# First layer: where the scale and shift rows lie, and when two experts' down weights are loaded

## The reference, cut to what matters

```python
hx = hx + g1x * merge_branches(..., w_out[l])          # output projection, gated residual
u  = rmsnorm(hx, norm2_g[l]) * (1 + sc2x) + sh2x       # scale and shift rows
hb = silu(xb @ w_gate[e]) * (xb @ w_up[e])             # xb: the rows of u given to expert e
y  = (hb @ w_down[e]) * weight
hx = hx + g2x * y
```

## Time and profile before

| what | value |
|---|---|
| median of the runs | 2652.45 us (2652.15 to 2654.38, 3 runs) |
| the profiled execution's own time | 2659.47 us |
| its span (first to last instruction) | 2657.7 us |
| TensorE busy / VectorE busy | 2424.9 us (91%) / 1075.4 us (40%) |
| bytes moved by DMA | 588.27 MB |
| mean granted TensorE clock | 0.979 |

### The profile page before, as it was taken

The page is one execution under the profiler, slowest core; times in us unless marked ns, Lnnn a source line. Parts: engine busy times, 40 slices in busy tenths (PEclk is TensorE's granted clock), DMA queues, the critical chain, the costliest instruction groups (busy, mean ns, idle before and its releaser), DMA issues. The chain is left out here.

```text
span 2657.7 us, 35289 instructions
## 1 busy us (share of the span) xinstructions
PE 2424.9 (91%) x12944; PEld 1516.8 (57%) x12944; DVE 1075.4 (40%) x2132; ACT 622.3 (23%) x1369; POOL 691.2 (26%) x644
## 2 busy tenths in 40 slices
PE   7989988999999999988887899989999999988887
PEld 2445665455555566555554568645787555555553
DVE  5764477444221573111111165854432732322222
ACT  3441222343111232221111142334211311111111
POOL 0003222465231002222222223246531022222221
PEclk8999999999999999999999999999999999999999
DMA  9873030020222529999999913112135689999996
GB/s 365 343 316 137 1 121 19 13 55 1 67 53 87 228 112 361 392 400 401 402 394 385 357 68 113 40 32 55 37 83 178 257 333 393 391 408 407 401 403 246
DMA packets 190670, 588.27 MB, mean 221 GB/s; under 512 B 47376, under 2 KB 109115, under 8 KB 134108
## 3 DMA queue, kind: packets, MB, share of 16 engines
q1 hardware_dynamic: 166053, 551.86, 54.9%
q0 software_dynamic: 22400, 29.42, 3.4%
q10 hardware_dynamic: 2103, 5.51, 0.5%
HBM read 581.31 MB, written 51.51 MB: 238 GB/s over the span
## 5 line engine op out<-in xcount | busy, mean ns | idle before, releaser
L2624 PE MATMUL ps<-w,moe_xt 128*64 128x256 f32 x2816 | 338.3, 394 | 64.4 <-DMA w<-in_w_up_e 61.9
L2764 POOL DMA_INDIRECT rows_out<-moe_rows_out,table x128 | 118.0, 922 | 740.2 <-DVE moe_rows_out L2829 373.9
L2624 PEld LDWEIGHTS ps<-w,moe_xt 128*64 128x64 f32 x2816 | 218.8, 141 | 153.2 <-issue 70.6
L2879 DVE TENSOR_TENSOR moe_gated<-ps,moe_gated 64x256 f32<-64x256 f32 x128 | 54.5, 426 | 504.2 <-ACT moe_gated L2848 504.1
L2848 ACT ACTIVATE moe_gated<-ps 64x256 f32<-64x256 f32 x128 | 48.2, 376 | 668.7 <-PE ps L2624 668.7
L2624 PE MATMUL ps<-early_w,moe_xt 128*64 128x256 f32 x1280 | 151.4, 390 | 31.9 <-DMA early_w<-in_w_up_e 31.8
L1673 POOL TENSOR_SCALAR attn_p<-attn_p,attn_rs 128x768 f32<-128x768 f32 (+1 forms) x80 | 155.4, 1950 | 81.4 <-DVE attn_rs L1847 80.9
L2632 PE MATMUL ps<-w,moe_ht 128*64 128x512 f32 x704 | 170.4, 604 | 2.3 <-issue 2.3
L2145 PE MATMUL ps<-w_out,mix 128*128 128x512 f32 x320 | 144.6, 602 | 7.0 <-PEq L150 7.0
L2865 DVE TENSOR_TENSOR moe_rows_out<-ps,moe_row_gate 64x512 f32<-64x512 f32 x128 | 88.1, 688 | 138.0 <-PE ps L2632 136.0
L2624 PEld LDWEIGHTS ps<-early_w,moe_xt 128*64 128x64 f32 x1280 | 101.3, 140 | 68.3 <-issue 36.6
(11 more groups left out here) (429 smaller groups left out, 4260.5 us busy)
## 6 DMA issues: line engine op xcount, KB each, us to landing
w<-in_w_gate_e SPq DMA_DIRECT2D x88, 1024.0 KB, 25.5
w<-in_w_up_e SPq DMA_DIRECT2D x88, 1024.0 KB, 29.5
w<-in_w_down_e SPq DMA_DIRECT2D x88, 1024.0 KB, 29.3
prep_w<-in_w_ada SPq DMA_DIRECT2D x24, 2048.0 KB, 14.3
early_w<-in_w_gate_e SPq DMA_DIRECT2D x40, 1024.0 KB, 25.5
early_w<-in_w_up_e SPq DMA_DIRECT2D x40, 1024.0 KB, 29.6
early_w<-in_w_down_e SPq DMA_DIRECT2D x40, 1024.0 KB, 29.8
w_merge<-in_w_in SPq DMA_DIRECT2D x32, 512.0 KB, 5.4
```

Source lines behind the costliest of these rows:

```text
L2624: last = nc.tensor.matmul(ps[k * SLOTS:(k + 1) * SLOTS, 0:DE], xt[:, c], wgu[:, k, c], start=c == 0, stop=c == KC - 1)
L2764: nc.gpsimd.indirect_dma_start(out=dram["y"], out_offset=bass.IndirectOffsetOnAxis(ap=m.table[0:SLOTS, j:j + 1], axis=0), in_=y[:, j % 2], ...
L2879: nc.vector.tensor_tensor(h[:, b % 2], m.ps[SLOTS:2 * SLOTS, b % 2, 0:DE], sg[SLOTS:2 * SLOTS, b % 2], ALU.mult).then_inc(s["h_done"], 1)
```

## The change

The out stage's tile `g` is split: the gate row stays in a small tile `gate`, and the scale and shift rows move into a tile `rows` that lies at the top of memory, over the fourth slot. In the first layer that slot now is an early one: its down weights are loaded once the last product by `w_out` is done, its gate and up weights once VectorE has used the rows for the last time (`utok_done`). The down weights of slots 4 and 5, which the out stage loaded after `u_out`, are issued at the start of the moe stage in both layers, and SP's wait for `g1` is gone. TensorE gets 26 instead of 16 `keep_warm` calls at the end of the out stage, and in the moe stage 6 ahead of the first transposes and 4 behind them instead of 4 ahead.

```diff
@@ out_stage, SP
-                    sp.dma_start(s["g"][:, t, k], of(t)).then_inc(s["rows_in" if k else "gates_in"], 16)
+                    sp.dma_start(rows[:, t, k - 1] if k else s["gate"][:, t], of(t)).then_inc(s["rows_in" if k else "gates_in"], 16)
...
             sp.wait_ge(s["mm_done"], 2 * NT)
             freed(sp, 0)
-            sp.wait_ge(s["u_out"], 16 * NT)
+            sp.wait_ge(s["utok_done"], NT)
             freed(sp, 1)
@@ out_stage, TensorE, its end
             lists(NT - 1)
-            keep_warm(nc, m, 0, 16)
+            keep_warm(nc, m, 0, 26)
@@ out_stage, VectorE (gate, gained, rows)
-    ... s["g"][:, t, 0, cols(half)] ... s["g"][:, t, 1, cols(half)] ... s["g"][:, work[j][0], 2]
+    ... s["gate"][:, t, cols(half)] ... rows[:, t, 0, cols(half)] ... rows[:, work[j][0], 1]
@@ moe_stage, SP
-            sp.wait_ge(s["g1"], 16)
             first_loads(sp)
             next_gate_up(RU, 0)
@@ moe_stage, TensorE
+            keep_warm(nc, m, 7, 6)
+            x_transposes(0, 0, 0)
             keep_warm(nc, m, 7, 4)
-            x_transposes(0, 0, 0)
             rounds(pe, body, late_lists)
@@ experts
             def freed_loads(sp, k):
                 if k == 0:
+                    for b in range(early, FREED_EXPERTS):
+                        load_down(sp, a, l, b, slots[b], down_in[b])
                     load_gate_up(sp, a, l, FREED_EXPERTS, slots[FREED_EXPERTS], gu_in[FREED_EXPERTS])
                 else:
-                    for b in (FREED_EXPERTS, RU - 1):
-                        load_down(sp, a, l, b, slots[b], down_in[b])
+                    for b in range(early, FREED_EXPERTS):
+                        load_gate_up(sp, a, l, b, slots[b], gu_in[b])
+
+            def last_downs(sp):
+                for b in (FREED_EXPERTS, RU - 1):
+                    load_down(sp, a, l, b, slots[b], down_in[b])
...
+                rows = until_rows.enter_context(nc.sbuf_tensor(f"out_rows{l}", [P, len(streams), 2, D], F32, side="right"))
...
-        moe_stage(..., lambda sp: first_round(sp, range(early, FREED_EXPERTS)), (xg_at, xg, gathered), out)
+        moe_stage(..., last_downs, (xg_at, xg, gathered), out)
```

More of the change, by code:

```diff
@@ L2093, in out_loads, with out_stage @@
         eng.dma_start(w[:, g], w_out[l].rearrange("(c p) n -> p c n", p=P)[:, :, g * 4 * P:(g + 1) * 4 * P]).then_inc(loaded[g], 16)
-def out_stage(nc, m, l, dram, streams, early, picks, first_rows, gathered, router_loads, then, freed_tiles, freed):
+def out_stage(nc, m, l, dram, streams, early, picks, first_rows, gathered, rows, router_loads, then, freed_tiles, freed):
     work = [(t, at // P + j) for t, at, n in streams for j in range(n // P)]
@@ L2308, in gate @@
                     dve.wait_ge(s["added"], done)
-                nc.vector.tensor_tensor(s["t"][:], m.ps[:, 2 * (j % 2) + half], s["g"][:, t, 0, cols(half)], ALU.mult).then_inc(s["prod_done"], 1)
+                nc.vector.tensor_tensor(s["t"][:], m.ps[:, 2 * (j % 2) + half], s["gate"][:, t, cols(half)], ALU.mult).then_inc(s["prod_done"], 1)
                 dve.wait_ge(s["prod_done"], done + 1)
@@ L2328, in gained, with finished_rows @@
                 dve.wait_ge(s["added"], 2 * j + half + 1)
-                nc.vector.tensor_tensor(s["utok"][:, cols(half)], m.resid[:, tile, cols(half)], s["g"][:, t, 1, cols(half)], ALU.mult).then_inc(s["gained"], 1)
-            def rows(j):
+                nc.vector.tensor_tensor(s["utok"][:, cols(half)], m.resid[:, tile, cols(half)], rows[:, t, 0, cols(half)], ALU.mult).then_inc(s["gained"], 1)
+            def finished_rows(j):
                 dve.wait_ge(s["gained"], 2 * j + 2)
-                nc.vector.scalar_tensor_tensor(s["utok"][:], s["utok"][:], s["r"][:, j:j + 1], s["g"][:, work[j][0], 2], ALU.mult, ALU.add).then_inc(s["utok_done"], 1)
+                nc.vector.scalar_tensor_tensor(s["utok"][:], s["utok"][:], s["r"][:, j:j + 1], rows[:, work[j][0], 1], ALU.mult, ALU.add).then_inc(s["utok_done"], 1)
             def constants():
@@ L2437, in _ @@
                 root(j)
-                rows(j)
+                finished_rows(j)
             selection(NT - 1)
@@ L3115, in experts @@
                 picks[name] = until_moe.enter_context(nc.sbuf_tensor(f"pick_{name}{l}", shape, F32))
-            for b in range(FREED_EXPERTS, RU):
+            for b in range(early, RU):
                 slot_at[b] = top - (RU - b) * SLOT * 4
@@ L3132, in experts @@
             gathered = nc.alloc_semaphore(f"first_rows_in{l}")
-            out_stage(nc, m, l, dram, streams, out_early, picks, xg, gathered, lambda sp: router_loads(sp, l, a, consts, picks),
-                      lambda sp: first_round(sp, range(early)), freed_tiles, freed_loads)
+            with ExitStack() as until_rows:
+                rows = until_rows.enter_context(nc.sbuf_tensor(f"out_rows{l}", [P, len(streams), 2, D], F32, side="right"))
+                assert early == FREED_EXPERTS or nc.sbuf_top == slot_at[early]
+                out_stage(nc, m, l, dram, streams, out_early, picks, xg, gathered, rows, lambda sp: router_loads(sp, l, a, consts, picks),
+                          lambda sp: first_round(sp, range(early)), freed_tiles, freed_loads)
             late.close()
@@ L3141, in experts @@
         homes = blend_homes(nc, l, slot_at, base, top, out is not None)
-        moe_stage(nc, m, l, a, dram, (slots, gu_in, down_in), homes, streams, picks, lambda sp: first_round(sp, range(early, FREED_EXPERTS)), (xg_at, xg, gathered), out)
+        moe_stage(nc, m, l, a, dram, (slots, gu_in, down_in), homes, streams, picks, last_downs, (xg_at, xg, gathered), out)
     return None if out is not None else {"at": (base, top), **{name: homes[name] for name in ("u", "w_hy", "w_hy_in")}}
```

2 lines of the change are left out of this document (1 added, 1 removed).

## The result

The changed kernel's median is 2658.61 us over 12 runs (2652.46 to 2664.73), beside 2653.03 us for the kernel before over 12 runs (2650.16 to 2658.46). The ratio is 1.0019, with a 95% interval of 1.001 to 1.0028: 5.0 us slower, between 2.7 and 7.4. The forecast was 2649.2, 3.25 us faster, in a range up to 2654.5. In a second timing the changed kernel gave 1.0014 (0.9999 to 1.0028).

What follows compares the result with a forecast made beforehand. Each moe stage was taken to end with its stream of loads. First layer 2.2 - 0.2 = 2.0, second 2.6 - 1.35 = 1.25, total 3.25 us gained: 2652.45 becomes 2649.2, range 2645.0 to 2654.5.

Steps and rivals of the forecast that it cites:

- the price of the moved down loads: Moe stage's start: expert 1's gather lands behind the down loads, stalling TensorE 0.2 us in the first layer, 1.35 in the second.
- the gather of 2121.44: Kernel before, second layer: expert 0's gather, landing 7.45 us behind the down loads' issue; the row used to price expert 1's gather.
- the holes behind the stream's start: First layer: the load queue runs dry by about 0.2 and 0.5 us behind expert 6's gate, 0.7 in the sum.
- 7.85 us of bytes: First layer: expert 3's three loads, 3.146 MB, leave the moe stage's stream, worth 7.85 us at 401 GB/s.
- The first layer's boundary: Out stage to moe stage: ten more warm-up calls, 2.4 us, move it from 996.07 to 998.5, TensorE arriving last.
- The first load of the stream: First layer's moe stage: expert 6's gate is issued at 1005.85 instead of 1000.87, 4.98 us later.
- The second layer's boundary: Out stage to moe stage: without the down loads, expert 0's gather lands sooner; boundary at 2126.1 instead of 2126.92.
- rival C: Gather for expert 1 costs its upper bound, stalls of 2.6 and 2.8 us; 0.6 us lost, 2653.0; chance 0.15.
- B's first half: Gather for expert 1 is never late; no stall adds 1.55 us to the gain, 2647.6; whole rival's chance 0.25.
- B's second half: TensorE's clock doesn't fall in the first layer's warm-up calls, adding 1.6 us, 2647.6; whole rival's chance 0.25.
- D: First layer's last store and expert 0's gather stick in 5.24 MB; boundary 7.5 us later, 2656.7; with E, chance 0.10.
- E: Stream isn't the bound; removed bytes give nothing, TensorE's later start costs 3.1 us in the first layer; with D, chance 0.10.

Runs made afterwards that it cites:

- slot-only kernel: Changed kernel with the down loads of slots 4 and 5 back in the out stage in both layers and the previous kernel's warm-up calls; ratio 1.0018.
- warm-up as before: Changed kernel with the warm-up calls of the kernel before (16 at the out stage's end, 4 ahead of the first transposes, none behind); ratio 1.0003.
- the kernel with the wait put back: Changed kernel with SP again waiting for the gather for expert 1 before it issues the two down loads; ratio 0.9999.
- warm-up-only kernel: Kernel before with only the warm-up calls of the changed kernel; ratio 1.0014.
- the down loads alone: Kernel before with only the two down loads moved to the moe stage's start and SP's wait for the gather removed; ratio 1.002.

## Why the prediction was wrong

**The step that failed** is the price of the moved down loads: "I take the 0.2 and 1.35, since here the loads ahead are two and not a full queue." The stalls were 2.1 to 2.5 us in the first layer and 2.6 to 3.1 in the second, over four profiles. That is about the upper bounds of that part, 2.6 and 2.8. I had the right mechanism and put it behind the wrong row: the gather of 2121.44 is alone in its queue, while behind the boundary three gathers are issued within 4 us. All three were held up and went together, so the first of them landed 9.6 us behind the boundary and not 7.45, and in the second layer 9.95 and not 8.6.

The traces have the lone case four times, a gather for expert 0 issued 2.1 to 2.4 us behind the two down loads, and it took 5.1 to 5.7 us. The first of three gathers, issued 2.2 us behind them, took 7.0 to 7.6. That the two others delay the first one's landing is argued from this and from the packet counts and was not tried by itself. Another cause is possible in the second layer, where expert 6's loads are issued at 2131.01, ahead of the landing at about 2133.6; in the first layer SP's queue had a share of only 10% from 1003 to 1004.

The stall works through a second term of the sum, the holes behind the stream's start, which I had put at 0.7 us. In the first profile the hole from 1010 on alone is 2.3 us (3 us at a share of 0.24). In the second, where the clock also fell, it is 4.8:

```profile
1012.00:1018.00 6.00, 6.00 (x38) 3.48 (x34) 5.26 (x7) 0.97 (x2) 0.00 (x0) 0.79 0.20 59
```

So of the 7.85 us of bytes 4.64 went to the later start, and the holes took most of the rest.

**A term was missing.** Behind a stall of 2 us and more TensorE's clock fell, and then expert 1's products took 1.3 to 2.4 us longer: in seven of the eight stretches. The rows of the kernel before had shown this after another wait (5.35 us), and I used that row only for what it gives back. Stall and fall together delay expert 7's loads. In the second layer they are issued at 102.4 on average before (101.9 to 103.3) and at 104.5 after (103.6 to 105.5), 2.1 us later, although the stage begins earlier; the stretch grew by 3.0.

**What was right.** The first layer's boundary: 2.4 us later was forecast, and it was 2.1 (127.03 against 124.93 behind the stage's start). The first load of the stream: 4.98 us later was forecast; counted from the stage's start it was 134.37 against 129.73, 4.64 (3.8 between the means of all profiles). The second layer's boundary is freed by the missing down loads, and GpSimd's gather is what holds a boundary (6.47 us in the slot-only kernel). The products of expert 0 ran 3.67 us in all four profiles and ended 2.8 us earlier in the first, 2.2 on average, where 2.6 was forecast. A stretch of the first layer does move with the stream's start (658.8 for 131.92, 656.6 for 129.73). But the sign that should have shown the gain went the other way: the first layer's last weight load was forecast 2 us earlier, and it is issued at 605.7 to 608.0 in the changed kernel's profiles, at 604.8 to 606.4 in those of the kernel before. With the stalls taken from the upper bounds the sum would have been rival C, 2653.0, and with the clock's fall of 2.4 and 1.5 us on top about 2657.

**The rivals.** C described what happened, but without the clock. B's first half is refuted: the gather did wait. The Trainium skill's page "DMA: Bandwidth & Descriptors", section "Queues, rings and completion order", has each DMA engine take turns between the queues that have work. In the first layer of this case's trace GpSimd's queue had no packet for some 4 us, until SP's loads were nearly at their end, so these rows speak against that rule at the scale of such a wait. In the second layer, once packets of the gathers moved, they did so beside SP's (2132 to 2133, packets, MB, share):

```profile
q1 hardware_dynamic: 37, 0.18, 95.4%
q0 software_dynamic: 169, 0.05, 23.2%
```

That part agrees with the rule; why the first packets came so late stays open. B's second half didn't occur in the first layer, and in the second the clock now fell in the longer calls in two of the four profiles (7.70 instead of 6.07 us). D didn't come: the store delayed the first gather by 1.3 us, and the calls covered it. The shorter calls of before didn't quite cover it: in the kernel "warm-up as before" the boundary came 1.7 us behind their end. E is out: with the same calls, the kernel with the wait put back, which has the early slot, took 656.5 us in its first stretch, and the warm-up-only kernel, which hasn't, 658.8.

**What stays open.** The stretches account for 3.9 of 5.0 us, within the interval. How much of that is the stall, and how much the clock, wasn't measured apart. Three kernels were timed slower than their stretches say: the longer warm-up alone at 3.7 us (0.5 to 6.9) with 0.1 in the stretches, the slot alone at 4.8 (0.5 to 9.3) with none, the down loads alone at 5.3 (2.1 to 8.8) with 1.7. Something outside the two stretches may cost time, or single profiles don't stand for the timed runs.

## What to carry to other kernels

Loads hidden behind a stage share their queue with the gather that ends it and with the first gathers of the next; before moving bulk, find each small transfer that is issued within some 6 us behind it (two loads of 1 MB held the queue that long here), and price it by rows with as many small transfers in flight. Where a stage ends with its loads, keep an account of bytes and holes: 7.85 us of bytes taken out gave nothing, because the start moved by 4.64 us and the stall opened holes behind it. A short stall on TensorE can have a second price, the clock, and it is paid by whatever waits for the next products.

## What the runs showed of the hardware

An indirect gather that takes 2.3 to 2.8 us in an idle queue took 7.1 to 8.0 in the changed kernel's four profiles, with only two 1 MB loads issued 1.2 to 2.2 us ahead of it and two more gathers behind it. That is as long as amid a full stream. A gather alone behind the same two loads took 5.1 to 5.7.

A stage boundary waits for GpSimd's gather: it came 0.4 us behind the landing in the second layer of the kernel before and in the first layer of the slot-only kernel.

In the same program the clock in a row of 26 equal warm-up calls fell in some executions and not in others: the row took 6.07 us in two of the changed kernel's profiles of the second layer and 7.70 in the two others. The 16 calls of the kernel before, 3.84 us in the earlier trace rows, took 5.46 and 5.37 there in its two further profiles, so a price read from one profile can be that of one execution.

And two executions of the same kernel differ ahead of anything that was changed. The first `w_out` product lies at 865.8, 866.0 and 871.1 us in the three profiles of the kernel before. The first two were taken on one chip, but on one chip it also lay at 859.9 in one of these kernels and at 871.6 in another. So a span is not to be compared with a span.
